# A fused two-layer encoder: 296 of its 128x128 transposes taken from TensorE and done by VectorE in 32x32 blocks

## Chip, cores, metric

One core of one Trainium2 chip runs the whole program in one launch. The metric is device time in microseconds (us).

## The reference

Two layers over x (256 tokens x 2048, float32) and a memory of 256 tokens. In each:

```python
h = rms_norm(x, norm_mix);  z = h @ w_in       # gates, u, v, q, k, v, memory q in one projection
y_sgu  = u * (sgu_w @ rms_norm(gelu(v)) + sgu_b)              # 4 groups x 128
q, k   = rope(rms_norm(q)), rope(rms_norm(k))                 # 8 query heads, 2 kv heads, 128 wide
y_attn = softmax(q k^T * 128**-0.5) v
y_mem  = softmax(mq mk^T * 128**-0.5) mv                      # 4 heads; mk, mv = rms_norm(mem) @ w_mem_kv
y = sum_i sigmoid(g_i + gate_b_i) * (branch_i @ w_br_i);  x = x + y @ w_out
a, b = split(rms_norm(x) @ w_gate_up);  x = x + (silu(a) * b) @ w_down     # inner width 5632
```

## The kernel before

**Products.** All weights come as one stream of units of 1 MB (4 k-tiles of 128 rows x 512 columns), loaded by SyncE into four slots of `raw` (L252 to L256). Precision comes from splitting each operand into two parts of type float32r: ScalarE copies half a unit (a *half*, 2 k-tiles) to `w_hi` (`split`, L575), VectorE subtracts it from the raw weights into `w_lo` (`split`, L839), TensorE forms hi x hi, hi x lo and lo x hi for two token blocks: 12 matmuls of 128x128 by 512 a half (`half`, L332). `w_hi` and `w_lo` have four slots; the split of half n+4 waits until TensorE has used half n. A *chunk* is the k-tiles of 512 output columns, 8 halves where k is 2048, summed in one of three PSUM accumulators of two banks. The layer's order of chunks is: two of the memory projection, six of `w_in` (u, v, kv, memory q, the two halves of the query heads), four gate chunks of the first branch and one of the second, then for each 512 columns of y one more gate chunk, the branch products (2, 2 and 4 halves) and a gate chunk; `w_out` (4 chunks); the feed-forward in parts of 4, 4 and 3 groups of 512 inner columns (two chunks a group), each part followed by its `w_down` (4 chunks of 2 halves a group).

**Transposes.** Activations are computed with tokens on the partitions, and the next product needs features there. `transposes` (L362) waits until the single PSUM tile `tr` (four blocks by 256 tokens) is free, lets TensorE multiply up to eight 128x128 blocks of float32 by the identity, and signals `tr_done`. ScalarE then copies `tr` out (`op_plain`, `op_gain`, `turn_out`) and, where the product needs both parts, VectorE forms the low part and signals `tr_free` (L859, L868). Names: mk and mq are keys and queries of the memory branch, u the result of the gating branch, kv the keys, `R_Q` and `R_Q + 1` the two halves of the query heads, `R_MQ` also the feed-forward's inner rows, `y_rows` y. What TensorE may read when is given by `need` in `chunk` (L349): ahead of a half it waits for `tr_free`.

**Order.** Each engine has one program written out by hand, in which `split(n)` stands between the other work; all waits are on counting semaphores. An engine does nothing past a wait, so VectorE's other work stands in front of its next split, and ScalarE's copy of `tr` in front of its own. VectorE's program by stage: the memory keys L1018 to L1042; u, kv, mq and q L1078 to L1116; the head pipeline L1118 to L1135 (maximum, reciprocal, low part of the output; the exponential is ScalarE's and the scaling GpSimd's, L289); gates and branches of y L1141 to L1186; `w_out` L1187; feed-forward L1205 to L1253. VectorE takes results out of an accumulator after `chunk_done`, which waits for TensorE.

Of the kernel before, what the change touches and what calls it, by code (L numbers as in the profile page):

```python
# [30 lines left out]
P = 128  # L31
# [3 lines left out]
TB = SEQ // P  # L35
HD = 128
# [5 lines left out]
N_BRANCH = 3  # L42
# [19 lines left out]
PART = 4  # L62
LAST = ACT_GROUPS - 2 * PART
SEED = float(0x5F3759DF)

# [71 lines left out]
def trunk(nc, weights, x_in, mem_in, memT_in, vecs_in, gains_in, sguT_in, rope_in, bias_in, out):  # L137
    with ExitStack() as ctx:
# [189 lines left out]
        def _(pe):  # L328
# [60 lines left out]

            def head_scores(a):  # L390
                if a >= 2:

                    pe.wait_ge(exp_done, n.at("head", -1))
                for t in range(TB):
                    tok = slice(t * P, (t + 1) * P)
                    if a < N_MEM:
                        q_, k_ = mem_qT[:, a, tok], mem_kT[:, a, :]
                    else:
                        q_, k_ = qT[:, a - N_MEM, tok], kT[:, (a - N_MEM) // GROUP, :]
                    mm = pe.matmul(scores[:, a % 2, t * SEQ:(t + 1) * SEQ], q_, k_, start=True, stop=True)  # L400
                mm.then_inc(scored, 1)
                n.add("head")
# [41 lines left out]
            with n.loop(DEPTH, half=2 * N_UNITS, tr=TR_LAYER, rows=ROWS_LAYER, acc0=ACC_LAYER, acc1=ACC_LAYER,  # L444
# [14 lines left out]

                chunk(0, *A, upto=1, need={0: 3})  # L460
                wait_rows()
                transposes(rows_at(R_MK))
                chunk(0, *A, first=1, need={2: 3, 4: 2, 6: 1})

# [10 lines left out]

                chunk(1, *A, upto=1)
                wait_rows()
                transposes(rows_at(R_U))
                chunk(1, *A, first=1)

                chunk(0, *A, upto=2)
                wait_rows()
                transposes(rows_at(R_KV), N_KV)
                chunk(0, *A, first=2, upto=4)
                wait_taken(1)
                transposes(rows_at(R_MQ))
                chunk(0, *A, first=4)

                chunk(1, *A, upto=7)
                wait_rows()  # L490
                transposes(rows_at(R_Q))
                chunk(1, *A, first=7)

# [26 lines left out]
                chunk(0, *B, halves=2)  # L520
                pe.wait_ge(rows_ready, n.at("rows"))
                transposes(y_at(0))
                chunk(1, *B, halves=2, kt=4)
                transposes(y_at(1))
                chunk(2, *B, halves=4, kt=8, upto=2)
                transposes(y_at(2))
                chunk(2, *B, halves=4, kt=8, first=2)

# [16 lines left out]
                def inner(groups):  # L545
                    with n.loop(groups - 1, half=2 * FULL, acc0=1, acc1=1, tr=1):
                        chunk(1, *A)
                        chunk(0, *A, upto=2)
                        wait_taken(1)
                        transposes(rows_at(R_MQ))  # L550
                        chunk(0, *A, first=2)
                    chunk(1, *A)

                def down(groups):
                    halves = 2 * groups
                    chunk(0, *B, halves=halves, upto=2, need={0: 0})
                    wait_taken(1)
                    transposes(rows_at(R_MQ))
                    chunk(0, *B, halves=halves, first=2, need={halves - 2: 0})
                    for c in range(1, NC):  # L560
                        chunk(c % 2, *B, halves=halves)
# [10 lines left out]
        def _(act):  # L572
# [87 lines left out]
            with n.loop(DEPTH, half=2 * N_UNITS, tr=TR_LAYER, acc0=ACC_LAYER, acc1=ACC_LAYER, acc2=NC,  # L660
# [58 lines left out]
                n.add("acc1")  # L719
                split(6)  # L720
                turn_out(kT[:, :, :], blocks=N_KV)
                split(2)
                turn_out(mem_qT[:, :, :], vecs[:, V_MQ:V_MQ + 1])
# [75 lines left out]
                def inner(groups):  # L799
                    with n.loop(groups - 1, half=2 * FULL, acc0=1, acc1=1, tr=1) as j:  # L800
                        split(4)
                        sigmoid_inner()
                        split(4)
                        n.add("acc1")
                        split(6)
                        op_plain(b_hi[:, kts(j), :])
                        split(2)
                    split(4)
                    sigmoid_inner()
                    split(4)  # L810
# [21 lines left out]
        def _(dve):  # L832
# [26 lines left out]
            def op_gain(hi, lo, kt0, gain):  # L859

                wait_hi()
                for k in range(kt0, kt0 + 4):
                    last = dve.scalar_tensor_tensor(out=lo[:, k, :], in0=tr[:, k - kt0, :],  # L863
                                                    scalar=vecs[:, gain + k:gain + k + 1],
                                                    in1=hi[:, k, :].bitcast(F32), op0=ALU.mult, op1=ALU.subtract)
                last.then_inc(tr_free, 1)

            def op_plain(kt):  # L868
# [120 lines left out]
            with n.loop(DEPTH, half=2 * N_UNITS, op=OPS_LAYER, acc0=ACC_LAYER, acc1=ACC_LAYER, acc2=NC,  # L989
                        head=N_HEADS, inv=N_HEADS, sums=2 + NC, sig=SIG_LAYER, bias0=N_BRANCH * NC // 2,  # L990
                        bias1=N_BRANCH * NC // 2, layer=1) as layer:
# [38 lines left out]
                dve.drain()  # L1030
                head_norm(R_MK).then_inc(rows_ready, 1)

# [6 lines left out]
                rsqrt(rs_x, ss_x, D).then_inc(rs_ready, 1)  # L1039
                split(2)  # L1040
                take_scaled(1, mem_v[:, :, :], rs_mem)
# [37 lines left out]
                for g in range(SGU_G):  # L1079
# [3 lines left out]
                                                    in1=u_, op0=ALU.add, op1=ALU.mult)  # L1083
                last.then_inc(rows_ready, 1)
                split(2)
                take_scaled(0, rows[:, R_KV, :, :], rs_x)
# [9 lines left out]
                split(1)  # L1096
                rotate(R_KV, R_V, R_Q, 2, N_KV).then_inc(rows_ready, 1)
                split(1)

                split(4)  # L1100
                take_scaled(1, rows[:, R_MQ, :, :], rs_x)
                dve.drain()
                split(1)
                head_sums(R_MQ, R_V)
                split(1)
                rsqrt(q_scale[:, 0, :, :].rearrange("p t h -> p (t h)"), ss[:, 0:8], HD, SCALE)
                split(2)

# [5 lines left out]
                split(1)  # L1114
                rotate(R_Q, R_V, R_TMP, 0, 4).then_inc(rows_ready, 1)
                split(1)  # L1116

                for s in range((NC + 1) * FULL):  # L1118
                    split(1)
                    if s == 4:  # L1120
                        wait_taken(1)
                        head_sums(R_Q + 1, R_V)
                    if s == 5:
                        rsqrt(q_scale[:, 2, :, :].rearrange("p t h -> p (t h)"), ss[:, 0:8], HD, SCALE)
                    if s == 6:
                        rotate(R_Q + 1, R_V, R_Q, 0, 4).then_inc(rows_ready, 1)
                    if s >= FULL + 3 and s % FULL == 3:
                        c = s // FULL - 1
                        take_gate(c % 2, y_rows[:, :, columns(c)], c)
# [10 lines left out]

                def gates(c):  # L1141

                    yc = y_rows[:, :, columns(c)]
                    split(4)
                    take_gate(0, rows[:, R_U, :, :], 4)
                    split(7)
                    take_gate(1, rows[:, R_V, :, :], 5, lead=3)
                    split(3)
                    wait_sig()
                    dve.tensor_tensor(yc, yc, acc[0][:, :, :], ALU.mult).then_inc(taken[0], 1)  # L1150
                    n.add("acc0")
# [19 lines left out]
                c = NC - 1  # L1171
                gates(c)
                op_plain(slice(0, 4))
                split(2)
                wait_sig()
                branch(1, R_V, c)
                op_plain(slice(4, 8))

                split(2)
                op_plain(slice(8, 12))  # L1180
                split(2)
                chunk_done()
                branch(2, R_U, c).then_inc(rows_ready, 1)
                split(3)
                op_plain(slice(12, 16))
# [34 lines left out]
                def inner(groups):  # L1220
                    with n.loop(groups - 1, half=2 * FULL, acc0=1, acc1=1, op=1, sig=1) as j:
                        gate_inner()
                        split(4)
                        chunk_done()
                        take_inner(1, R_MQ)
                        split(2)
                        op_plain(kts(j))
                        split(2)
                    gate_inner()

                def down(groups):
                    split(4)
                    chunk_done()
                    take_inner(1, R_MQ)
                    split(2)
                    op_plain(kts(groups - 1))
# [7 lines left out]
                with n.loop(2, half=2 * PART * FULL + NC * 2 * PART, acc0=PART + 2, acc1=PART + 2, op=PART,  # L1244
                            sig=PART):
                    inner(PART)
# [15 lines left out]

ROWS_LAYER = 6 + NC
HALVES_Y = 2 * FULL + 2 + 2 + 4
# [61 lines left out]
```

## Time and profile before

| | |
|---|---|
| device time, 3 runs | median 2800.63 us (2800.22 to 2801.59) |
| profiled execution, first to last instruction | 2800.6 us |
| busy: TensorE, VectorE, ScalarE, GpSimd | 99%, 56%, 45%, 2% |
| VectorE's splits (L846) | 976, 1194.3 us busy |
| ScalarE's splits (L585) | 976, 1034.6 us busy |
| TensorE's transposes through L368 | 456, 272 ns each as shown, overlapping |
| granted TensorE clock, mean | 0.997 |
| DMA | 191 GB/s on average |

Busy is the time in which an engine has an instruction under way; matmuls overlap, so the count times the mean is more than the span. In a timeline each row gives the start, the length from the first start to the last end of the instructions merged in it, and in brackets the idle time before it with what ended it.

### The profile page before, as it was taken

The numbers are of one execution on the slowest core, as the hardware profiler recorded it, in microseconds if no ns is written. First come the engines' busy times: TensorE is split into PE (matmuls) and PEld (weight loads), VectorE is DVE, ScalarE is ACT, GpSimd is POOL, SyncE is SP. The second block draws the span as 40 slices with busy tenths as digits, with TensorE's granted clock in tenths as the row PEclk, the third lists the DMA queues.
The fourth block names the chain that finished last, engine by engine and source line by source line (L and its number), as shares of the span: only waits on it lengthen the run. The fifth ranks groups of instructions, "written<-read, shape, count | busy, mean of one in ns | idle before, by whom it ended". The sixth has DMA issues, their size and how long they took to land.

```text
span 2800.6 us, 34813 instructions
## 1 busy us (share of the span) xinstructions
PE 2772.3 (99%) x12476; PEld 2297.9 (82%) x12476; DVE 1576.3 (56%) x1771; ACT 1263.5 (45%) x1408; POOL 51.5 (2%) x74
## 2 busy tenths in 40 slices
PE   7999999999999999999999999999999999999999
PEld 5888888888888888888878888888888888888887
DVE  6676555565555455555576755555655555554554
ACT  5445444444443344344364455444444443443443
POOL 0001100000000000000000010000000000000000
PEclk9999999999999999999999999999999999999999
DMA  7544455555555555555555544555555555555553
GB/s 289 195 179 156 170 198 204 197 211 189 187 194 189 188 189 187 194 195 184 192 211 191 184 158 177 200 194 199 211 192 182 193 195 183 194 187 190 193 191 139
DMA packets 76457, 535.63 MB, mean 191 GB/s; under 512 B 8720, under 2 KB 8720, under 8 KB 13104
## 3 DMA queue, kind: packets, MB, share of 16 engines
q1 hardware_dynamic: 71776, 515.99, 51.3%
q0 software_dynamic: 4560, 17.96, 2.0%
q8 instruction: 84, 1.38, 0.2%
q14 instruction: 37, 0.30, 0.0%
HBM read 531.81 MB, written 2.10 MB: 191 GB/s over the span
## 4 chain that ended last, share of the span: by engine, by line
PE 96%; DVE 1%; DMA 1%; issue 1%; ACT 1%; DVEq 1%; POOL 0%; SPq 0%; ACTq 0%; POOLq 0%
PE acc L343 31%; PE acc L345 31%; PE acc L344 31%; PE tr L368 2%; DMA raw<-weights 1%; PE tr L432 1%; PE acc L400 1%; PE tr L415 0%; DVE w_lo L846 0%; DMA y<-memT_in 0%; ACT w_hi L585 0%; DVEq L971 0%; ACT b_hi L671 0%; DVEq L901 0%; ACT rows L658 0%
## 5 line engine op out<-in xcount | busy, mean ns | idle before, releaser
L846 DVE TENSOR_TENSOR w_lo<-raw,w_hi 128x1024 fp32r<-128x1024 f32 x976 | 1194.3, 1226 | 1174.4 <-ACT w_hi L585 1169.9
L585 ACT ACTIVATE w_hi<-raw 128x1024 fp32r<-128x1024 f32 x976 | 1034.6, 1061 | 1492.6 <-PE acc L345 1481.9
L343 PE MATMUL acc<-w_hi,a_hi 128*128 128x512 f32 x2560 | 1005.0, 393 | 3.0 <-issue 3.0
L345 PE MATMUL acc<-w_hi,a_lo 128*128 128x512 f32 x2560 | 996.6, 389 | 0.0
L344 PE MATMUL acc<-w_lo,a_hi 128*128 128x512 f32 x2560 | 996.3, 389 | 0.0
L344 PEld LDWEIGHTS acc<-w_lo,a_hi 128*128 128x128 f32 x2560 | 480.8, 188 | 101.9 <-issue 3.4
L345 PEld LDWEIGHTS acc<-w_hi,a_lo 128*128 128x128 f32 x2560 | 480.6, 188 | 100.3
L343 PEld LDWEIGHTS acc<-w_hi,a_hi 128*128 128x128 f32 x2560 | 480.7, 188 | 99.1 <-DVE w_lo L846 0.7
L343 PE MATMUL acc<-w_hi,b_hi 128*128 128x512 f32 x1344 | 527.3, 392 | 14.3 <-DVE b_lo L998 14.3
L344 PE MATMUL acc<-w_lo,b_hi 128*128 128x512 f32 x1344 | 524.6, 390 | 0.0
L345 PE MATMUL acc<-w_hi,b_lo 128*128 128x512 f32 x1344 | 524.4, 390 | 0.0
L343 PEld LDWEIGHTS acc<-w_hi,b_hi 128*128 128x128 f32 x1344 | 253.3, 188 | 67.8 <-issue 16.1
L345 PEld LDWEIGHTS acc<-w_hi,b_lo 128*128 128x128 f32 x1344 | 253.3, 188 | 53.1
L344 PEld LDWEIGHTS acc<-w_lo,b_hi 128*128 128x128 f32 x1344 | 253.3, 188 | 51.6
L1208 DVE SCALAR_TENSOR_TENSOR rows<-acc,stats,rows 128x512 f32<-128x512 f32 x88 | 61.7, 743 | 0.0
L957 DVE TENSOR_TENSOR x<-acc,x 128x1024 f32<-128x1024 f32 x33 | 40.2, 1218 | 9.5 <-PE acc L345 8.6
L871 DVE TENSOR_TENSOR b_lo<-tr,b_hi 128x1024 fp32r<-128x1024 f32 (+1 forms) x32 | 38.9, 1217 | 0.0
L368 PEld LDWEIGHTS tr<-ident,rows 128*128 128x128 f32 x264 | 30.8, 140 | 4.4
L368 PE MATMUL tr<-ident,rows 128*128 128x128 f32 x264 | 34.3, 272 | 0.0
L607 ACT ACTIVATE b_hi<-tr 128x1024 fp32r<-128x1024 f32 (+1 forms) x32 | 32.6, 1019 | 0.0
L863 DVE SCALAR_TENSOR_TENSOR a_lo<-tr,vecs,a_hi 128x256 fp32r<-128x256 f32 x64 | 26.5, 476 | 1.9 <-ACT a_hi L601 1.9
L794 ACT ACTIVATE rows<-acc,stats 128x512 f32<-128x512 f32 x44 | 27.4, 674 | 0.0
(92 smaller groups left out, 659.8 us busy)
## 6 DMA issues: line engine op xcount, KB each, us to landing
raw<-weights SPq DMA_DIRECT2D x488, 1024.0 KB, 4.8
y<-memT_in POOLq DMA_DIRECT2D x12, 512.0 KB, 7.0
bias<-bias_in POOLq DMA_DIRECT2D x24, 256.0 KB, 4.8
rows<-mem_in POOLq DMA_DIRECT2D x2, 2048.0 KB, 13.0
x<-x_in SPq DMA_DIRECT2D x1, 2048.0 KB, 18.8
out<-x SPq DMA_DIRECT2D x4, 512.0 KB, 5.0
qT<-sguT_in POOLq DMA_DIRECT2D x2, 256.0 KB, 13.1
qT<-gains_in POOLq DMA_DIRECT2D x2, 192.0 KB, 14.7
```

What stands on the lines that cost most here:

```text
L343: pe.matmul(o, hi[:, kt + k, tok], wh, start=first and k == 0, stop=False)
L344: pe.matmul(o, hi[:, kt + k, tok], wl, start=False, stop=False)
L345: mm = pe.matmul(o, lo[:, kt + k, tok], wh, start=False, stop=last and k == HALF_KT - 1)
L368: tp = pe.transpose(tr[:, b, t * P:(t + 1) * P], src(b, t), ident[:, :])
L400: mm = pe.matmul(scores[:, a % 2, t * SEQ:(t + 1) * SEQ], q_, k_, start=True, stop=True)
L432: mm = pe.matmul(oT_ps[:, a % 2, :], v_, probT(a)[:, k, :], start=k == 0, stop=k == TB - 1)
L585: act.activation(w_hi[:, h % SPLIT_SLOTS, :], raw[:, slot, part * HALF:(part + 1) * HALF], ACT.Copy).then_inc(hi_ready, 1)
L607: act.activation(hi, tr[:, :, :], ACT.Copy).then_inc(op_hi, 1)
L846: dve.tensor_tensor(w_lo[:, h % SPLIT_SLOTS, :], raw[:, slot, part * HALF:(part + 1) * HALF], w_hi[:, h % SPLIT_SLOTS, :].bitcast(F32), AL ...
L871: dve.tensor_tensor(b_lo[:, kt, :], tr[:, :, :], b_hi[:, kt, :].bitcast(F32), ALU.subtract).then_inc(tr_free, 1)
L957: last = dve.tensor_tensor(xc, acc[acc_i][:, :, :], xc, ALU.add)
L1208: last = dve.scalar_tensor_tensor(out=rows[:, r, t, :], in0=acc[acc_i][:, t, :], scalar=rs_ffn[:, t:t + 1], in1=rows[:, R_U, t, :], op0=AL ...
```

## The change

`turn_rows` lets VectorE do the transposes of mk, u, kv, mq, the first half of the query heads, the first three 512-column blocks of y, and all eleven groups of the feed-forward's inner rows. It issues four instructions a part, one to each quadrant of 32 source partitions; an instruction turns, for both token blocks and all (4, or for kv 2) feature blocks, one 32x32 block each and writes it to the quadrant `part` of `tr`. Four parts make a block; the last signals `tr_done`, and the first waits for `tr_free`. TensorE keeps the transposes of x, of the last block of y, of the second half of the query heads and of the probabilities. The parts stand between VectorE's splits. TensorE's chunks lose their breaks, counters follow, and TensorE waits for `tr_free` ahead of the first head's scores. ScalarE copies kv out three splits earlier, and the inner rows two later in the loops. Only changed lines are shown:

```diff
@@ -61,6 +61,8 @@
+SQ = 32
+QUADS = P // SQ
@@ -388,6 +390,9 @@
+                if a == 0:
+                    pe.wait_ge(tr_free, n.at("tr", 1))
@@ -457,10 +462,8 @@
-                chunk(0, *A, upto=1, need={0: 3})
-                wait_rows()
-                transposes(rows_at(R_MK))
-                chunk(0, *A, first=1, need={2: 3, 4: 2, 6: 1})
+                chunk(0, *A, need={0: 3, 2: 2, 4: 1, 6: 0})
+                n.add("tr")
@@ -473,23 +476,10 @@
-                chunk(1, *A, upto=1)
-                wait_rows()
-                transposes(rows_at(R_U))
-                chunk(1, *A, first=1)
-                chunk(0, *A, upto=2)
-                wait_rows()
-                transposes(rows_at(R_KV), N_KV)
-                chunk(0, *A, first=2, upto=4)
-                wait_taken(1)
-                transposes(rows_at(R_MQ))
-                chunk(0, *A, first=4)
-                chunk(1, *A, upto=7)
-                wait_rows()
-                transposes(rows_at(R_Q))
-                chunk(1, *A, first=7)
+                chunk(1, *A)
+                chunk(0, *A)
+                chunk(1, *A)
+                n.add("tr", 4)
@@ -518,13 +508,9 @@
-                pe.wait_ge(rows_ready, n.at("rows"))
-                transposes(y_at(0))
...
-                transposes(y_at(1))
-                chunk(2, *B, halves=4, kt=8, upto=2)
-                transposes(y_at(2))
-                chunk(2, *B, halves=4, kt=8, first=2)
+                chunk(2, *B, halves=4, kt=8)
+                n.add("tr", NC - 1)
@@ -545,18 +531,15 @@
-                        chunk(0, *A, upto=2)
-                        wait_taken(1)
-                        transposes(rows_at(R_MQ))
-                        chunk(0, *A, first=2)
+                        chunk(0, *A)
+                        n.add("tr")
...
-                    chunk(0, *B, halves=halves, upto=2, need={0: 0})
-                    wait_taken(1)
-                    transposes(rows_at(R_MQ))
-                    chunk(0, *B, halves=halves, first=2, need={halves - 2: 0})
+                    chunk(0, *B, halves=halves, upto=halves - 2, need={0: 0})
+                    n.add("tr")
+                    chunk(0, *B, halves=halves, first=halves - 2, need={halves - 2: 0})
@@ -717,9 +700,9 @@
-                split(6)
+                split(3)
...
-                split(2)
+                split(5)
@@ -802,9 +785,8 @@
-                        split(6)
+                        split(8)
...
-                        split(2)
@@ -864,6 +846,22 @@
+                n.add("tr")
+            def rows_of(r, blocks=4):
+                return rows[:, r, :, 0:blocks * HD]
+            def turn_rows(src_, part, blocks=4):
+                if part == 0:
+                    dve.wait_ge(tr_free, n.at("tr", 1))
+                    n.add("tr")
+                for pq in range(QUADS):
+                    src = src_[pq * SQ:(pq + 1) * SQ, :, :].rearrange("p t (k f i) -> p t k f i", f=QUADS, i=SQ)
+                    dst = tr[part * SQ:(part + 1) * SQ, 0:blocks, :].rearrange("p k (t q i) -> p t k q i", t=TB, q=QUADS)
+                    last = dve.transpose(dst[:, :, :, pq, :], src[:, :, :, part, :])
+                if part == QUADS - 1:
+                    last.then_inc(tr_done, 1)
@@ -987,7 +985,7 @@
-                        head=N_HEADS, inv=N_HEADS, sums=2 + NC, sig=SIG_LAYER, bias0=N_BRANCH * NC // 2,
+                        head=N_HEADS, inv=N_HEADS, sums=2 + NC, sig=SIG_LAYER, tr=TR_LAYER, bias0=N_BRANCH * NC // 2,
@@ -1028,7 +1026,7 @@
-                head_norm(R_MK).then_inc(rows_ready, 1)
+                head_norm(R_MK)
@@ -1037,7 +1035,12 @@
-                split(2)
+                turn_rows(rows_of(R_MK), 0)
+                split(1)
+                turn_rows(rows_of(R_MK), 1)
+                split(1)
+                turn_rows(rows_of(R_MK), 2)
+                turn_rows(rows_of(R_MK), 3)
@@ -1081,8 +1084,13 @@
-                last.then_inc(rows_ready, 1)
-                split(2)
+                dve.drain()
+                turn_rows(rows_of(R_U), 0)
+                split(1)
+                turn_rows(rows_of(R_U), 1)
+                split(1)
+                turn_rows(rows_of(R_U), 2)
+                turn_rows(rows_of(R_U), 3)
@@ -1094,17 +1102,27 @@
-                rotate(R_KV, R_V, R_Q, 2, N_KV).then_inc(rows_ready, 1)
-                split(1)
+                rotate(R_KV, R_V, R_Q, 2, N_KV)
+                dve.drain()
+                turn_rows(rows_of(R_KV, N_KV), 0, N_KV)
+                turn_rows(rows_of(R_KV, N_KV), 1, N_KV)
+                split(1)
+                turn_rows(rows_of(R_KV, N_KV), 2, N_KV)
+                turn_rows(rows_of(R_KV, N_KV), 3, N_KV)
...
-                split(1)
+                turn_rows(rows_of(R_MQ), 0)
+                split(1)
+                turn_rows(rows_of(R_MQ), 1)
...
+                turn_rows(rows_of(R_MQ), 2)
...
-                split(2)
+                split(1)
+                turn_rows(rows_of(R_MQ), 3)
+                split(1)
@@ -1112,11 +1130,17 @@
-                rotate(R_Q, R_V, R_TMP, 0, 4).then_inc(rows_ready, 1)
+                rotate(R_Q, R_V, R_TMP, 0, 4)
+                dve.drain()
+                turn_rows(rows_of(R_Q), 0)
+                turn_rows(rows_of(R_Q), 1)
...
+                    if s == 0:
+                        turn_rows(rows_of(R_Q), 2)
+                        turn_rows(rows_of(R_Q), 3)
@@ -1124,6 +1148,7 @@
+                        n.add("tr")
@@ -1138,12 +1163,15 @@
-                def gates(c):
+                def gates(c, turned=None):
...
-                    split(7)
+                    for k in range(7):
+                        split(1)
+                        if turned is not None and k < QUADS:
+                            turn_rows(turned, k)
@@ -1169,18 +1197,29 @@
-                gates(c)
+                gates(c, y_rows[:, :, columns(0)])
...
-                split(2)
+                turn_rows(y_rows[:, :, columns(1)], 0)
+                split(1)
+                turn_rows(y_rows[:, :, columns(1)], 1)
+                split(1)
+                turn_rows(y_rows[:, :, columns(1)], 2)
+                turn_rows(y_rows[:, :, columns(1)], 3)
...
-                split(2)
+                turn_rows(y_rows[:, :, columns(2)], 0)
+                split(1)
+                turn_rows(y_rows[:, :, columns(2)], 1)
+                split(1)
+                turn_rows(y_rows[:, :, columns(2)], 2)
+                turn_rows(y_rows[:, :, columns(2)], 3)
...
+                n.add("tr")
@@ -1218,21 +1257,31 @@
-                    with n.loop(groups - 1, half=2 * FULL, acc0=1, acc1=1, op=1, sig=1) as j:
+                    with n.loop(groups - 1, half=2 * FULL, acc0=1, acc1=1, op=1, sig=1, tr=1) as j:
...
-                        split(2)
+                        dve.drain()
+                        for part in range(QUADS - 1):
+                            turn_rows(rows_of(R_MQ), part)
+                            split(1)
+                        turn_rows(rows_of(R_MQ), QUADS - 1)
+                        split(1)
...
-                        split(2)
...
-                    split(2)
+                    dve.drain()
+                    turn_rows(rows_of(R_MQ), 0)
+                    split(1)
+                    turn_rows(rows_of(R_MQ), 1)
+                    turn_rows(rows_of(R_MQ), 2)
+                    split(1)
+                    turn_rows(rows_of(R_MQ), 3)
@@ -1242,7 +1291,7 @@
-                            sig=PART):
+                            sig=PART, tr=PART):
@@ -1260,7 +1309,7 @@
-ROWS_LAYER = 6 + NC
+ROWS_LAYER = 2 + NC
...
```

## Rows read from the trace of the kernel before

**Rows 1.** The page, part 1: busy us, share of the span, instructions.
```profile
PE 2772.3 (99%) x12476; PEld 2297.9 (82%) x12476; DVE 1576.3 (56%) x1771; ACT 1263.5 (45%) x1408; POOL 51.5 (2%) x74
```

**Rows 2.** TensorE's waits: line, released by; us in total, times, longest.
```profile
PE acc L343 <- DVE b_lo L998: 14.3, 2, 12.1
...
PE tr L415 <- POOL rows L292: 0.4, 2, 0.2
```

**Rows 3.** Timeline of ScalarE at w_down's start: start us, us, instruction [idle before <-releaser].
```profile
2735.46 1.06 ACT L585 ACTIVATE w_hi<-raw 128x1024 fp32r<-128x1024 f32 x1 [1.66 <-PE acc L345]
2736.42 1.01 ACT L607 ACTIVATE b_hi<-tr 128x1024 fp32r<-128x1024 f32 x1
```

**Rows 4.** Timeline of TensorE, same place.
```profile
2735.26 1.03 PE L368 MATMUL tr<-ident,rows 128*128 128x128 f32 x8
2736.05 0.48 PE L343 MATMUL acc<-w_hi,b_hi 128*128 128x512 f32 x1
2736.36 0.40 PE L344 MATMUL acc<-w_lo,b_hi 128*128 128x512 f32 x1
```

**Rows 5.** Timeline of VectorE, mk's stage of the first layer.
```profile
73.04 2.36 DVE L846 TENSOR_TENSOR w_lo<-raw,w_hi 128x1024 fp32r<-128x1024 f32 x2
...
76.64 1.21 DVE L846 TENSOR_TENSOR w_lo<-raw,w_hi 128x1024 fp32r<-128x1024 f32 x1
77.77 0.41 DVE L1048 TENSOR_TENSOR turn<-rope,qT 128x256 f32<-128x256 f32 x1
78.11 0.62 DVE L1055 TENSOR_TENSOR turn<-rope,qT 128x64 f32<-128x64 f32 x4
```

**Rows 6.** Timeline of VectorE, u and kv.
```profile
134.49 1.65 DVE L1082 SCALAR_TENSOR_TENSOR rows<-acc,vecs,rows 128x256 f32<-128x256 f32 x4
...
144.40 1.22 DVE L871 TENSOR_TENSOR b_lo<-tr,b_hi 128x1024 fp32r<-128x1024 f32 x1
...
147.12 1.23 DVE L846 TENSOR_TENSOR w_lo<-raw,w_hi 128x1024 fp32r<-128x1024 f32 x1
...
152.33 1.23 DVE L846 TENSOR_TENSOR w_lo<-raw,w_hi 128x1024 fp32r<-128x1024 f32 x1
...
155.78 3.49 DVE L846 TENSOR_TENSOR w_lo<-raw,w_hi 128x1024 fp32r<-128x1024 f32 x3
```

**Rows 7.** Timeline of ScalarE, mk's stage.
```profile
74.25 1.06 ACT L585 ACTIVATE w_hi<-raw 128x1024 fp32r<-128x1024 f32 x1 [1.66 <-PE acc L345]
```

**Rows 8.** Timeline of ScalarE, stage of u.
```profile
136.72 1.06 ACT L585 ACTIVATE w_hi<-raw 128x1024 fp32r<-128x1024 f32 x1 [3.40 <-PE acc L345]
```

**Rows 9.** Timeline of VectorE, mq and the first half of the query heads.
```profile
167.04 1.22 DVE L900 TENSOR_TENSOR rows<-rows 128x1024 f32<-128x1024 f32 x1
...
169.70 1.22 DVE L846 TENSOR_TENSOR w_lo<-raw,w_hi 128x1024 fp32r<-128x1024 f32 x1
...
173.86 2.36 DVE L846 TENSOR_TENSOR w_lo<-raw,w_hi 128x1024 fp32r<-128x1024 f32 x2
...
198.18 0.68 DVE L918 TENSOR_TENSOR rows<-rows,turn 128x512 f32<-128x512 f32 x1
...
202.09 4.63 DVE L846 TENSOR_TENSOR w_lo<-raw,w_hi 128x1024 fp32r<-128x1024 f32 x4
```

**Rows 10.** Timeline of ScalarE, last chunk of y.
```profile
564.87 1.06 ACT L585 ACTIVATE w_hi<-raw 128x1024 fp32r<-128x1024 f32 x1 [0.21 <-PE acc L345]
```

**Rows 11.** Timeline of VectorE, last chunk of y.
```profile
570.96 1.22 DVE L871 TENSOR_TENSOR b_lo<-tr,b_hi 128x1024 fp32r<-128x1024 f32 x1
...
576.16 1.21 DVE L1156 TENSOR_TENSOR rows<-rows,acc 128x1024 f32<-128x1024 f32 x1
...
578.61 1.22 DVE L871 TENSOR_TENSOR b_lo<-tr,b_hi 128x1024 fp32r<-128x1024 f32 x1
```

**Rows 12.** Timeline of VectorE where the last w_down begins.
```profile
2732.25 1.40 DVE L1208 SCALAR_TENSOR_TENSOR rows<-acc,stats,rows 128x512 f32<-128x512 f32 x2
```

**Rows 13.** Stretch: length, busy PE, PEld, DVE, ACT, POOL, clock, DMA share, GB/s.
```profile
1411.00:1414.30 3.30, 3.30 (x9) 2.54 (x8) 1.82 (x3) 0.57 (x2) 0.74 (x2) 0.51 0.94 372
```

## The prediction

> **What bounds the kernel now.** I read the page's busy line first, then TensorE's waits, then its order in time, and VectorE last, since the change takes work off the one and puts it on the other. TensorE is busy 99% of the span, VectorE 56% [rows 1]. Almost nothing holds TensorE up: 14.3 us in two waits where the layers begin, 0.4 us for the first probabilities [rows 2]. So an instruction that leaves TensorE shortens the time as long as nothing new is late. What can be late is the split of the weights. TensorE takes one half (12 matmuls) each 2.72 us: ScalarE's split of a later half follows it, 1.06 busy and 1.66 waiting [rows 3]. ScalarE and VectorE split four halves ahead, and ScalarE's split of half n+4 begins 0.20 us after TensorE has gone over to what follows half n (2735.46 against 2735.26 [rows 3, 4]), so the due time of every half can be read from ScalarE's rows.
>
> **What goes.** Eight transposes begin at 2735.26, the next matmul at 2736.05, and that one takes 0.31 to the next instead of 0.227 (2.72/12) [rows 4]. A group of eight costs 0.79 + 0.09 = 0.88 us. Per layer go mk, u, kv (four blocks), mq, q, three of y and eleven of the feed-forward: 148 transposes, 296 in all, 37 groups' worth. **Gain: 37 x 0.88 = 32.6 us**, all of it on the path.
>
> **What comes.** Each group becomes 16 VectorE transposes of 32 partitions by 256 elements (128 for kv), in four parts of four. No row of before has this operation, nor VectorE writing PSUM. Nearest rows, from start to next start (VectorE's instructions overlap by some 0.08): 128x256 within SBUF 0.34 (77.77 to 78.11) [rows 5]; 128x256 with PSUM at one end, four in 1.65 less 0.08, 0.39 [rows 6]. Lower bound: the marginal price of an element (1.14 for 1024, 0.34 for 256: 1.04 ns) with no fixed part, 0.27. Upper: each element passes twice, 0.39 + 0.27 = 0.66. I take 0.39, the nearest, since one end is PSUM: a part P is 1.56 us, a kv part 1.56 - 4 x 0.133 = 1.03. That is some 600 instructions and 230 us, and VectorE would stand at 65%; the average says nothing of the places where VectorE already works without a pause.
>
> The Vector Engine (DVE) Microarchitecture Reference of the Trainium skill, section 3.8, says that the 32x32 array fills by columns before it drains by rows, at one element per cycle and lane. No row here shows it. By that, 32 elements more on 0.34, one would take 0.37, an estimate, and the sum below would be some 4 us less. VectorE: DVE Perf Modes of the Trainium skill speaks against the change in "Rules for kernel authors": a 128x128 transpose belongs on TensorE if PSUM may take it. The trace agrees: 0.11 us of TensorE a block here, 0.78 of VectorE by my price.
>
> **The walk.** I follow VectorE's program through each stage. An instruction starts when the one before it is through and its input is there; a split takes 1.14 (2.36 for two, less overlap [rows 5]) and TensorE can use it 0.09 later. Halves are counted from the layer's start.
>
> *mk.* The two splits from 73.04 on are halves 18 and 19. Half 17 starts at 74.05 [rows 7], so half 20 is due at 82.2. New order: P, split 18, P, split 19, P, P, mem_v (1.32: 75.32 to 76.64), split 20: 73.04 + 4 x 1.56 + 2.28 + 1.32 + 1.23 = 84.1 [rows 5]. TensorE waits 1.9, and 0.2 more at half 21, before which the turn tables stand. **2.1 a layer.**
>
> *u, kv, mq, q.* Half 39 starts at 136.5 [rows 8], half 46 without transposes is due at 155.6. VectorE: u ready at 134.49 + 1.65 + drain 0.1 = 136.24; P, split 42, P, split 43, P, P: 144.76; kv taken 146.18; split 44 147.32; lo of u and head sums (144.40 to 147.12: 2.72) 150.04; split 45 151.18; rsqrt and norm (148.26 to 152.33: 4.07) 155.25; split 46 usable at 156.5, **0.9 late**. Rotation (153.47 to 155.78) and drain 158.8, two kv parts 160.86; split 47 usable at 162.1, due 159.2: **2.9**. After two more parts split 48 is **0.5** late [rows 6]. Splits 49 to 51 and the taking of mq end at 170.03; P, split, P, head sums (2.66), split 53, P, rsqrt (3.02) bring split 54 to 183.9, due 181.6: **2.3**. VectorE catches up; split 60 ends at 194.5, then sums, split, rsqrt, split, rotation and drain (4.01): 206.4; P, P; split 63 usable at 210.8, due 208.4: **2.4** [rows 9]. Two more parts and the second rotation push back the first maximum, exponential, inverse and scaling, for which TensorE waited 0.2 a layer before, so there is no slack [rows 2]. At that rotation's end VectorE is 7.9 later than before, TensorE 5.6 (9.0 of waits, less 3.4 of transposes): **2.3** more. Sum **11.3 a layer**. Behind it the heads run with pauses, as before.
>
> *y.* E is the first half of the last gate chunk. Half E+9 starts at 564.67 [rows 10], E+16 is due at 583.7. y of chunk 0 is turned one part to a split, each with 1.5 us of pause: nothing; without that cover 6 us. From 570.96 on: lo of y0 1.14; P, split, P, split, P, P; branch 1 (576.16 to 578.61: 2.45), lo of y1 1.13, P, split E+16: 572.1 + 5 x 1.56 + 7.1 = 587.0, **3.3** late [rows 11]. ScalarE meanwhile stands in its copy of y1, with splits E+16 and E+17 queued behind it, until the fourth part is there. Then P, split E+17, P, P, ScalarE's copy of y2 1.1 [rows 3] with split E+18 behind it, lo of y2: split E+18 at 583.8 + 8 x 1.56 = 596.3, due 592.4: **3.9**. Branch 2 makes TensorE's wait for y3 0.9. Sum **8.1 a layer**.
>
> *Feed-forward.* In its loops the parts stand one to a split, and the turned block is used a chunk or more later: nothing, covered by 1.5 us of pause a half; uncovered it would be 6.2 a group. Where w_down begins: 2732.25 + 1.42 + P + split + 2P + split + P = 2742.2, ScalarE's copy 1.1, lo 1.2: 2744.5 [rows 3, 12]. Half 2 of w_down starts at 2735.26 [rows 4]. Parts of four groups ask for the block at half 6 (2746.1): no wait. The part of three asks at half 4 (2740.7): **3.8 a layer**.
>
> *Clock.* Behind the shorter of the two waits of 14.3 (2.2 us) 3.3 us ran at a granted 0.51, the 1.2 GHz level, a loss of 1.7 [rows 2, 13]. Seven waits a layer would be 2.3 or more. Where VectorE is what is late, a slower TensorE only waits less afterwards; open is what follows the last of y (1.7 less 0.9) and w_down (1.7): **5 in all**. Weights have units of lead beyond the four halves, so SP's transfers stay hidden; POOL gets no new instruction.
>
> **Sum:** -32.6 + 2 x (2.1 + 11.3 + 8.1 + 3.8) + 5 = -32.6 + 50.6 + 5 = +23.0. The profiled execution's span, 2800.6, equals the median of the runs: 2824.
>
> **Rivals.**
> A. *The gain comes whole or nearly.* At 0.27 a transpose the same walk gives 0.2, 5.1, 4.2 and 2.0 us of waits, 23 in both layers: 2791. With none it is 2768. For it: 44% of VectorE is free. Against: every row of 256 elements takes 0.34 or more, and the free time isn't where many parts stand. It decides below 0.31 each, where waits and gain are equal. 0.15.
> B. *VectorE bounds the stages*, a transpose costing twice as much (0.66): waits of 6.4, 28.8, 16.7 and 16.3 a layer, 136 in all: 2905; at 0.50 it is 2853. For it: an unseen operation, into PSUM. Against: VectorE's rows differ little between operations. Above 0.44: 0.15.
> C. *The transposes cost TensorE nothing*, hidden between matmuls, so the change takes nothing off: 2857. Against: rows 4. 0.02.
> The forecast's case has 0.68, with 2800 to 2845 as its own range (0.31 to 0.44 each).
>
> **How the numbers follow.** 2824; the range reaches into A and B, 2796 to 2858. A measurement of this kernel tells 0.2%, 5.6 us, from no change. Faster than that: A's, and a little more, 0.16. Within: near 0.32 each, 0.08. Slower: the rest, 0.76.
>
> **What would show it.** Right: TensorE's transposes gone, and new waits of L343 on VectorE's split (L846) of 1 to 4 us, some ten a layer, in these four places and none in the feed-forward's loops; VectorE's transposes 0.42 to 0.48 us long (0.39 and the overlap); stretches at 1.2 GHz behind the waits. Wrong: transposes of 0.35 or shorter, or splits in time at halves 47, 54, 63 and E+16; then the time is under 2800. Waits in the feed-forward's loops would show B.

## The result and the profile after

The changed kernel takes 2857.84 us (median of 4, 2857.0 to 2858.34) against 2801.11 for the one before on the same chip: **ratio 1.0201, 95% interval 1.0189 to 1.0213, 57 us slower**. The forecast had 23 us slower, 2824, in a range of 2796 to 2858. The direction was right; the size was not, and the time lies at the very end of the range.

The page after, its busy line, clock and chain (before: [rows 1]):

```profile
PE 2770.7 (97%) x12180; PEld 2283.5 (80%) x12180; DVE 1846.7 (65%) x2379; ACT 1257.6 (44%) x1408; POOL 51.6 (2%) x74
...
PE 82%; DVE 10%; issue 3%; DVEq 2%; ACT 1%; DMA 1%; POOL 0%; SPq 0%; ACTq 0%; POOLq 0%
```

TensorE has 296 instructions fewer and yet nearly the same busy time, 2770.7 against 2772.3. VectorE stands at 65%, as forecast, and now holds 10% of the chain. The span grew from 2800.6 to 2856.6 (56.0). TensorE's idle time grew from 28.3 to 85.9 (57.6). The busy time should have fallen by 32.6 and fell by 1.6, which leaves 31 us to explain. Most of it is the clock: TensorE was busy for 61 us at a granted 0.50 (before: 8), and there one matmul follows the other after 0.427 us instead of 0.227, so these 53 us more cost some 25 (the mean granted clock is 0.986, before 0.997). The other 6 have no row of their own; a part is that the last matmul before each wait counts to its end (0.39) and not to the next start (0.227). In sum 57.6 + 31.0 - 32.6 = 56.0.

TensorE's waits after (line, releaser; us in total, times, longest; before: [rows 2]):

```profile
PE acc L345 <- DVE w_lo L828: 49.0, 19, 5.2
...
PE acc L345 <- DVE b_lo L996: 13.5, 2, 11.3
PE acc L345 <- DVE b_lo L869: 10.9, 2, 5.4
```

The wait of 13.5 at the layers' beginning is the old one (14.3). New are 49.0 us on VectorE's split of the weights and 10.9 on the low part of w_down's first block. Where they are, from the timeline of TensorE (first layer, then w_down and one in its second part):

```profile
85.64 0.50 PE L345 MATMUL acc<-w_hi,a_hi 128*128 128x512 f32 x1 [3.37 <-DVE w_lo L828]
...
162.21 0.50 PE L345 MATMUL acc<-w_hi,a_hi 128*128 128x512 f32 x1 [1.83 <-DVE w_lo L828]
...
168.55 0.50 PE L345 MATMUL acc<-w_hi,a_hi 128*128 128x512 f32 x1 [3.30 <-DVE w_lo L828]
...
192.49 0.53 PE L345 MATMUL acc<-w_hi,a_hi 128*128 128x512 f32 x1 [2.96 <-DVE w_lo L828]
...
221.94 0.50 PE L345 MATMUL acc<-w_hi,a_hi 128*128 128x512 f32 x1 [3.06 <-DVE w_lo L828]
...
252.66 0.65 PE L420 MATMUL tr<-ident,rows 128*128 128x128 f32 x4 [1.55 <-POOL rows L294]
...
608.39 0.80 PE L345 MATMUL acc<-w_hi,b_hi 128*128 128x512 f32 x1 [5.23 <-DVE w_lo L828]
...
618.78 0.50 PE L345 MATMUL acc<-w_hi,b_hi 128*128 128x512 f32 x1 [2.65 <-DVE w_lo L828]
...
898.26 0.50 PE L345 MATMUL acc<-w_hi,b_hi 128*128 128x512 f32 x1 [1.09 <-DVE w_lo L828]
...
1378.68 0.79 PE L345 MATMUL acc<-w_hi,b_hi 128*128 128x512 f32 x1 [5.43 <-DVE b_lo L869]
```

These are, in order, halves 20, 46, 47, 54 and 63, the first probabilities, halves E+16 and E+18, half 6 of w_down in a part of four, and half 4 in the part of three. Most are longer than forecast; shorter are the waits for the first probabilities and at E+18, and at halves 21 and 48, where the forecast had 0.2 and 0.5, and before the last block of y, where it had 0.9, there is none. VectorE by form (one instruction's mean in ns), and in time at the stage of u (before: [rows 6]):

```profile
L862 DVE STREAM_TRANSPOSE tr<-rows 32x256 f32<-32x256 f32 x480 | 218.9, 456 | 13.5 <-issue 5.6
...
L862 DVE STREAM_TRANSPOSE tr<-y 32x256 f32<-32x256 f32 x96 | 43.8, 456 | 1.7
...
L862 DVE STREAM_TRANSPOSE tr<-rows 32x128 f32<-32x128 f32 x32 | 10.3, 323 | 0.7
```

```profile
140.57 1.83 DVE L862 STREAM_TRANSPOSE tr<-rows 32x256 f32<-32x256 f32 x4 [0.15 <-issue]
142.42 1.23 DVE L828 TENSOR_TENSOR w_lo<-raw,w_hi 128x1024 fp32r<-128x1024 f32 x1
143.68 1.86 DVE L862 STREAM_TRANSPOSE tr<-rows 32x256 f32<-32x256 f32 x4
145.55 1.23 DVE L828 TENSOR_TENSOR w_lo<-raw,w_hi 128x1024 fp32r<-128x1024 f32 x1
```

One transpose is 0.456 long, within the forecast's 0.42 to 0.48. But nothing overlaps: four take 1.83 to 1.86, not 1.56, and the split before a part has 1.26 to itself (142.42 to 143.68) where before it had 1.14. A part with its split is 3.13 us, forecast 2.70; TensorE needs 2.72. And the clock behind the last wait (stretch: length, then busy PE, PEld, DVE, ACT, POOL, clock, DMA):

```profile
1378.70:1383.90 5.20, 5.20 (x12) 4.11 (x13) 2.12 (x2) 0.49 (x1) 0.00 (x0) 0.50 0.30 109
```

### The profile page after: what moved, and what is told of

The parts are those of the page before. It is cut to its first block, busy times and chain, and to the rows that moved or that the text cites. A ratio compares the mean times of both kernels' runs of the same rounds, so it can differ in the third digit from the quotient of the medians.

```text
span 2856.6 us, 34837 instructions
## 1 busy us (share of the span) xinstructions
PE 2770.7 (97%) x12180; PEld 2283.5 (80%) x12180; DVE 1846.7 (65%) x2379; ACT 1257.6 (44%) x1408; POOL 51.6 (2%) x74
## 4 chain that ended last, share of the span: by engine, by line
PE 82%; DVE 10%; issue 3%; DVEq 2%; ACT 1%; DMA 1%; POOL 0%; SPq 0%; ACTq 0%; POOLq 0%
PE acc L345 27%; PE acc L347 27%; PE acc L346 27%; DVE tr L862 4%; DVE w_lo L828 3%; DMA raw<-weights 1%; PE tr L437 1%; ACT w_hi L568 1%; DVEq L899 1%; PE acc L405 1%; DVE stats L900 0%; PE tr L420 0%; DVE a_lo L845 0%; PE tr L370 0%; ACT b_hi L590 0%
## 5 line engine op out<-in xcount | busy, mean ns | idle before, releaser
L862 DVE STREAM_TRANSPOSE tr<-rows 32x256 f32<-32x256 f32 (+1 forms) x512 | 229.2, 448 | 14.2 <-issue 5.6
L862 DVE STREAM_TRANSPOSE tr<-y 32x256 f32<-32x256 f32 x96 | 43.8, 456 | 1.7
```

The lines of the kernel that those rows point to most:

```text
L862: last = dve.transpose(dst[:, :, :, pq, :], src[:, :, :, part, :])
```

## The experiments

All but e1 and e5 start from the changed kernel and alter what is named; e1 is told against the kernel before, e5 against e1. The edits are shown condensed.

**e1, only the places with one part to a split.**

```diff
+ gates(c, y_rows[:, :, columns(0)])          # y of chunk 0
+ for part in range(QUADS - 1): turn_rows(rows_of(R_MQ), part); split(1)   # inner() only
  transposes(...) stay on TensorE for mk, u, kv, mq, q, y 1 and 2, and in down()
```

> VectorE turns only what stands one part to a split: the eight groups of the feed-forward's loops a layer and y of chunk 0. Theory (what a moved group costs is decided by its place, and a place with a pause of 1.5 us a half costs nothing although a part takes 1.87 us): 18 groups x 0.88 = 15.8 us less than before, 2785, and no wait of TensorE on VectorE's splits. Rival (VectorE's writes to PSUM or its mere load disturb TensorE wherever they are): the matmuls' period grows and the time is 2795 or more.

2783.0 us, ratio 0.9934 (0.9917 to 0.995): **faster than before by 18 us**. The page's busy line and the waits of TensorE:

```profile
PE 2755.2 (99%) x12332; PEld 2282.4 (82%) x12332; DVE 1706.0 (61%) x2059; ACT 1261.4 (45%) x1408; POOL 51.5 (2%) x74
```

```profile
PE acc L345 <- DVE b_lo L1014: 15.1, 2, 12.9
...
PE tr L420 <- POOL rows L294: 0.3, 2, 0.2
```

No wait on a split. TensorE's busy time fell by 17.1 for 18 groups, 0.95 each (forecast 0.88). So 288 VectorE transposes (131 us of work, by the same length of 456 ns) cost nothing that shows where they stand. (The profiled span fell by 19.3: besides the 17.1, the kernel before has two waits in the feed-forwards that name no releaser, 3.0 us together, and this run has none.) The rival is out.

**e2, y 1 and 2 back on TensorE; e3, w_down's first block back on TensorE.**

```diff
 # e2, TensorE; VectorE: n.add("tr"); split(2) in place of each block's parts
+transposes(y_at(1)); chunk(2, ..., upto=2); transposes(y_at(2)); chunk(2, ..., first=2)
 # e3, down()
-chunk(0, *B, halves=halves, upto=halves - 2, need={0: 0})
+chunk(0, *B, halves=halves, upto=2, need={0: 0}); wait_taken(1); transposes(rows_at(R_MQ))
```

> The changed kernel with the transposes of y's chunks 1 and 2 back on TensorE. By waits alone: 4 groups give back 3.5, the waits of 5.2 and 2.6 a layer go (15.6): 2846. Theory with the clock: the 1.2 GHz stretches behind them (4.1 and 3.4 us a layer, half of each lost, 7.5 in all) go as well: 2838. Rival (VectorE is what is late in any case and the clock's loss is absorbed, as forecast): 2846 or above.

> The changed kernel with the block that w_down begins with (three a layer) turned by TensorE again. By waits alone: 6 groups give back 5.3, waits of 5.43 + 2 x 1.09 a layer go (15.2): 2848. With the clock (5.2 us at 1.2 GHz behind the wait, 2.6 lost a layer): 2843.

e2: 2836.74, ratio 1.0125 (1.0108 to 1.0142), 21 us less than the changed kernel. e3: 2840.3, ratio 1.0138 (1.0121 to 1.0155), 17.5 less. Both are below what the waits alone give (2846 and 2848), and a little below the figures with the clock (2838 and 2843). TensorE is busy at a granted 0.50 for 41 us in e2 and 39 in e3, against 61 in the changed kernel. A wait takes more than its length.

**e4, half of every part.**

```diff
-for pq in range(QUADS):
+for pq in (0, QUADS - 1):
```

> The changed kernel with two of the four instructions of every part left out, so half of each block isn't turned. Theory (the waits are the length of VectorE's work in four places): a part takes 0.93 us and the walk of the prediction gives waits of 0, 3.6, 3.1 and 1.4 us a layer, 16 in all, 32.6 of gain: 2784 to 2790 with some clock. Rival (a fixed price of the hand-over, such as the copy of the tile or the semaphores, or PSUM writes as such): at most half of the 57 us goes, 2829 or more.

This kernel leaves half of each block unturned; it is there for its time alone. 2787.0, ratio 0.9951 (0.9934 to 0.9968), as its theory has it (2784 to 2790). The price of the change is the length of VectorE's parts; the hand-over of the tile, which is the same here, costs next to nothing.

**e5, mk and mq spread too.** Against e1:

```diff
-split(FULL)                       # VectorE, behind half 23
+for part in range(QUADS): split(1); turn_rows(rows_of(R_MK), part)
+split(FULL - QUADS)
-split(5)                          # behind half 55
+for part in range(QUADS): split(1); turn_rows(rows_of(R_MQ), part)
+split(1)
```

> VectorE turns the feed-forward's loops and y of chunk 0 as in the kernel that has only these, and also mk and mq, each moved to a stretch with one part to a split (mk behind halves 24 to 27, mq behind 56 to 59) and copied out by ScalarE accordingly later. u, kv, q, y 1 and 2, and w_down's first block stay on TensorE. Theory: 22 groups x 0.88 = 19.4 us less than before, 2781.5. Rival (mk's and mq's groups cost by themselves, not by place): above 2785.

2781.8, ratio 0.9931 (0.9914 to 0.9947), on another chip than e1 (0.9934, 0.9917 to 0.995): the two can't be told apart, and whether the four groups more gain their 3.5 us isn't shown. TensorE's busy time fell by 19.4 to 2752.9 for 22 groups, the forecast sum, but by only 2.3 against e1. A wait that names no releaser ("issue", about 0.65 in each feed-forward, 1.3 in all) stands where the kernel before has its 3.0 and e1 none. In the changed kernel mk cost 3.4 us of waiting a layer; here it costs none. Place decides, not the block.

```profile
PE 2752.9 (99%) x12300; PEld 2279.2 (82%) x12300; DVE 1735.1 (62%) x2123; ACT 1261.5 (45%) x1408; POOL 51.5 (2%) x74
```

**e6, TensorE busy while it would wait.**

```diff
+def fill(count):  # pe.matmul(acc[2][:, 0, :], ident, rope as 128x512), count times
 chunk(0, *A, upto=4, need={0: 3, 2: 2}); fill(3); chunk(0, *A, first=4, ...)   # mk
+if groups == LAST: fill(6)                                                     # w_down
```

> The changed kernel; where TensorE waits at half 20 (3.4 us) and at the last w_down (5.4 us), it first runs 3 and 6 matmuls of the identity by the rope tables into a free accumulator (0.85 us each), so it is busy while it would wait. Theory (each wait costs itself and then the 1.2 GHz stretch behind it): the waits' length stays in the time, the slow stretches behind these four waits go, 8 to 9 us less than the changed kernel: 2849. Rival (the clock's loss is absorbed by VectorE's lateness): no change, 2858.

2847.89, ratio 1.0167 (1.015 to 1.0184): 10 us less than the changed kernel, by adding work. The stretch of w_down and the page's busy line:

```profile
1372.00:1384.00 12.00, 11.74 (x43) 7.71 (x42) 7.34 (x10) 5.04 (x5) 0.00 (x0) 1.00 0.48 175
```

```profile
PE 2775.8 (98%) x12216; PEld 2282.5 (80%) x12216; DVE 1846.3 (65%) x2379; ACT 1257.3 (44%) x1408; POOL 51.5 (2%) x74
```

The granted clock there is 1.00 where it was 0.50 behind the bare wait. The 18 added matmuls (36 of the page's instructions) hold 16.1 us of busy time, by their group:

```profile
L385 PE MATMUL acc<-rope,ident 128*128 128x512 f32 x36 | 16.1, 592 | 0.0
```

Busy time grew by 5.1 only, so all other matmuls take 11.0 less; the idle time, 70.1 of a span of 2845.9, is 15.8 less than the changed kernel's 85.9. The rival (no change) is out. But not all of the 11 stood behind the four waits. In the changed kernel TensorE ran at 0.50 for 5.3 and 5.8 us behind the two of w_down and for 3.4 behind half 20 of the first layer; behind half 20 of the second, after the same wait of 3.37, it ran at 1.00:

```profile
1501.90:1505.30 3.40, 3.38 (x14) 2.62 (x15) 3.40 (x12) 1.71 (x3) 0.00 (x0) 1.00 0.00 0
```

At 0.47 us lost for each us at 0.50 (0.20 of 0.427) that is about 7. The other 4 are the balance of slow stretches behind waits that e6 hardly altered. Behind the old one of 2.19 us at the second layer's start the clock was low in the changed kernel and not in e6:

```profile
1438.10:1441.50 3.40, 3.40 (x9) 2.73 (x10) 2.56 (x5) 1.38 (x3) 1.44 (x3) 0.59 0.80 272
```

```profile
1433.70:1437.10 3.40, 3.40 (x15) 2.83 (x16) 2.52 (x5) 1.75 (x4) 1.39 (x3) 1.00 0.84 306
```

So a wait of 2.2 to 3.4 us brings a slow stretch in one execution and not in another; both layers' waits above 5 us brought one in the changed kernel. Of what the prediction said of mk, that the clock's loss there is absorbed, only the one slow stretch of the first layer is a test: TensorE's next wait, at half 46, ends 76.6 us after the one at half 20 in the changed kernel and 75.1 in e6, so the loss was passed on.

**e7 to e10, why a part is longer than forecast.** Each replaces the one instruction of `turn_rows`:

```diff
-last = dve.transpose(dst[:, :, :, pq, :], src[:, :, :, part, :])
+last = dve.tensor_copy(dst[:, :, :, pq, :], src[:, :, :, part, :])            # e7: a copy
+last = dve.transpose(scratch_in_sbuf, src[:, :, :, part, :])                  # e8: into SBUF
+last = dve.tensor_copy(tr[:, pq, :], src_[:, :, 0:HD])                        # e9: 128 partitions
+last = dve.tensor_copy(tr[pq * SQ:(pq + 1) * SQ, part, :], src_[same, :, 0:HD])  # e10: stays in its quadrant
```

> The changed kernel with each transpose replaced by a copy of the same 32x256 elements to the same place in PSUM, so nothing is turned. If the transpose itself costs more than the rows of before (0.39 from start to start): a copy has 0.39 or less, the time falls to about 2820. If the 32 partitions across quadrants or the write to PSUM do: the copy has 0.46 too and the time stays at 2858.

> The changed kernel with the transposes written to a small tile in SBUF (two slots, with a drain after the second instruction), so the products read stale blocks. If the write to PSUM makes them longer than the rows of before: single lengths fall from 0.456 to about 0.41. If it is the transpose: 0.456 stays.

> The changed kernel with each transpose replaced by a copy of 128 partitions x 256 elements into PSUM (nothing is turned; a drain behind the first three parts). The rows of 32 partitions in the changed kernel don't overlap with what follows them (start to start 0.466 at a length of 0.456), those of 128 partitions of before do, by 0.08. If the number of partitions or the quadrants decide: these copies overlap, 0.34 from start to start. If the write to PSUM decides: they don't, 0.42 or more.

> The changed kernel with each transpose replaced by a copy of 32 partitions x 256 elements that stays in its quadrant and writes one run of 256 in PSUM. If crossing quadrants or the pieces of 32 elements decide the missing overlap: start to start falls from 0.43 (the copies that cross) to 0.35. If 32 partitions or PSUM decide: 0.43 stays.

None of the four turns the blocks as the product needs them; they are there for their times. One run each: 2847.37, 2856.71, 2823.83 and 2849.77 us. e9 came out as one of its two cases (0.34 from start to start), e10 as the other (0.43 stays); e7 and e8 fell between theirs, so that neither the transposing nor PSUM explains the length by itself. By form, from e7, e8, e9 and e10:

```profile
L867 DVE COPY tr<-rows 32x256 f32<-32x256 f32 x480 | 203.4, 424 | 13.3 <-issue 5.6
```

```profile
L868 DVE STREAM_TRANSPOSE scratch<-rows 32x256 f32<-32x256 f32 x480 | 209.2, 436 | 20.9 <-issue 5.6
```

```profile
L865 DVE COPY tr<-rows 128x256 f32<-128x256 f32 x512 | 179.5, 419 | 8.1 <-issue 6.4
```

```profile
L865 DVE COPY tr<-rows 32x256 f32<-32x256 f32 x512 | 217.0, 424 | 14.0 <-issue 5.6
```

and in time, e9, then e10:

```profile
139.80 1.40 DVE L865 COPY tr<-rows 128x256 f32<-128x256 f32 x4
```

```profile
143.26 1.74 DVE L865 COPY tr<-rows 32x256 f32<-32x256 f32 x4
145.01 1.22 DVE L833 TENSOR_TENSOR w_lo<-raw,w_hi 128x1024 fp32r<-128x1024 f32 x1
```

Alone, a copy on 32 partitions (424 ns) is as long as one on 128 (419). But four of the latter end in 1.40, start to start 0.33; four of the former in 1.74, start to start 0.44, and what follows waits for the end. It is so with copies that stay in their quadrant and with those that cross, in runs of 256 and in pieces of 32, and 128-partition copies into the same PSUM tile do overlap.

Is it the width, then? In all the 32-partition versions each instruction also reads or writes in another quadrant (32 partitions) than the one before it. e8's trace parts the two, at y's chunk 0. All reads and writes here are in SBUF, and both transposes that follow a split read from partition 0 on, as the split does. The first also writes from partition 0 on, as the split does; the second writes to the next quadrant:

```profile
564.73 1.23 DVE L834 TENSOR_TENSOR w_lo<-raw,w_hi 128x1024 fp32r<-128x1024 f32 x1 [0.21 <-ACT w_hi L574]
565.87 1.83 DVE L868 STREAM_TRANSPOSE scratch<-y 32x256 f32<-32x256 f32 x4
567.72 1.23 DVE L834 TENSOR_TENSOR w_lo<-raw,w_hi 128x1024 fp32r<-128x1024 f32 x1
568.97 1.84 DVE L868 STREAM_TRANSPOSE scratch<-y 32x256 f32<-32x256 f32 x4
```

The first starts 1.14 us after its split, overlapped by 0.08 like any wide instruction; the second 1.25 after, with no overlap. It is the same in the second layer. In the changed kernel, where PSUM is written and VectorE's last write there had gone to another quadrant, the first has no overlap either (1.26). So not the width takes the overlap away. PSUM alone doesn't either (e9: a copy into PSUM stands 1.14 behind a split). What fits every row is that an instruction has no overlap when it reads or writes in another quadrant than VectorE's last read or write in that memory. For the write the rows above show it; for the read it is argued, since no run has two 32-partition instructions in a row on the same partitions.

On top the transpose is 32 ns longer than the copy, and PSUM 20 ns longer than SBUF. The array that fills before it drains (the Vector Engine (DVE) Microarchitecture Reference of the Trainium skill, section 3.8) would give an estimate of 33 ns, 32 elements at the 1.04 ns of the rows of before; the 32 ns agree.

e9 is also the forecast's own condition: 1.40 plus a drain of 0.15 is a part of 1.55 us, forecast 1.56, and its time is 2823.8, forecast 2824.

## Why the prediction was right and wrong

- **What goes, 32.6:** right, a little small. e1's 0.95 a group gives 35, e5's 0.88 gives 32.6.
- **What comes, 0.39 a transpose: the step that failed.** It took the overlap of 0.08, which the rows of before show between instructions that all start at partition 0, over to instructions each of which starts in another quadrant. Measured: 0.46 to 0.47 from start to start, and the neighbours lose their overlap too. The upper bound (0.66) held it; the value did not. The prediction's own figures, 2824 at 0.39 and 2853 at 0.50, give 2844 at 0.466: 20 of the missing 33 us. The other 13 are the clock, 26 more than its 5, less 13 us of waits that the same walk has too many.
- **The walk's places:** right, with one left out. TensorE waits at every half where it put 0.9 us or more, and nowhere in the feed-forward's loops. With the measured length its own formulas follow the trace: mk (halves 20 and 21), 4 x 1.86 - 4.1 = 3.3 (3.37, all at half 20); E+16, 5 x 1.86 - 4.5 = 4.8 (5.23); w_down's part of three, 4 x 1.86 - 2.4 = 5.0 (5.43). The part of four, in time by 1.6 in the forecast (2744.5 against 2746.1), is late by 1.09, four times. With the measured length its formula still leaves 0.4: the walk asked only for the block, and not for the split of the same half, which stands behind it in VectorE's program. The block is there at 897.07, the split at 898.23, and TensorE goes on at 898.26:

```profile
895.85 1.23 DVE L869 TENSOR_TENSOR b_lo<-tr,b_hi 128x1024 fp32r<-128x1024 f32 x1 [1.09 <-ACT b_hi L590]
897.00 3.48 DVE L828 TENSOR_TENSOR w_lo<-raw,w_hi 128x1024 fp32r<-128x1024 f32 x3
```

- **The wait at E+18:** the same formula gives 4.8 and 2.65 was measured, since TensorE was slow before it (4.1 us at a granted 0.50) and came later. That was the argument of the clock term, and here it holds.
- **Clock, 5: the second term that failed, by size.** The busy time shows 31 by remainder, of which some 25 by the granted clock. The argument that VectorE's lateness absorbs it holds only where VectorE is still behind at the next due half. At half 20 and in w_down it isn't: e6 gets about 7 us back there, of which the forecast had 3.4 (w_down). After 47 and 54 ScalarE's splits follow TensorE again before the next late half, so the loss is passed on; that part is read from the program's order, and no run took those waits apart.
- **Rival A** (the gain comes whole) was right for the places with pauses, which the prediction had at nothing: e1. **Rival B** had the right sign of the error: 0.466 lies beyond the 0.44 from which it was to decide, but the cost of a transpose rose by 0.08 and not by 0.27, and its sign, waits in the feed-forward's loops, did not come.
- How the 33 us between forecast and result part into length and clock: e9, at the forecast's length, has 2823.8 and still 7.4 + 29.0 us of waits on VectorE and a granted 0.991. The forecast's sum has 50.6 of waits, and in e9 TensorE's idle time grew by 37 (y has 5.2 a layer, forecast 8.1); it has 5 of clock, where e9's busy time leaves 17 (32.6 less 15.8). That these two errors cancel, and e9 meets 2824, is luck. All the rest came with the longer part, by longer waits and the slow stretches behind them.

## What to carry to other kernels

Work moved to an engine that is 44% idle is free only in places where the engine pauses at each step of the pipeline that it feeds: 22 groups there gave 19 us, 37 groups in all cost 57. Count the instruction with its real distance to the next one; the overlap seen between instructions on the same partitions doesn't carry over to a row of them that goes from quadrant to quadrant. Follow all that a half needs, the block and the split behind it. And where TensorE waits a few microseconds, add what the clock can take afterwards, unless something else is late by more than that.

## Unexpected of the hardware

- A VectorE copy on 32 partitions has the same length as on 128 (424 and 419 ns for 256 elements), but in a row that goes from quadrant to quadrant nothing overlaps: 0.44 against 0.33 from start to start. Where a 32-partition transpose starts at the same partitions as the instruction before it, it does overlap, by 0.08 (e8).
- Extra work in a waiting time can pay: 18 added matmuls took 10 us off (e6), about 7 of them by the granted clock of 1.00 instead of 0.50 behind the waits that they filled.
- After waits of the same 3.37 us at half 20, the granted clock was 0.50 for 3.4 us in the first layer and 1.00 in the second.
